# First stage in two sweeps with projections from split operands, and attention outputs folded in their own PSUM banks

## The chip, the core and the metric

The kernel runs on one core of a Trainium2 chip. The metric is the device time of one execution in microseconds (us). Five engines have a queue of instructions each and meet only at semaphores: TensorE (PE in the profile; PEld is its loading of the stationary operand), VectorE (DVE), ScalarE (ACT), GpSimd (POOL) and SyncE (SP), which here issues DMAs. An engine takes the instructions of its own queue in order.

## The reference

One encoder layer in float32, for 2048 tokens of width 1024. Only its first two parts matter here:

```
proj = x @ w_in                     # 1024 -> c_q 256, c_kv 128, k_r 32, and f, i, q, g of 512 each
# attention group: q = rms(c_q) @ w_uq, k and v = rms(c_kv) @ w_ukv, a rotary part of 32 shared by 8 heads,
#   softmax over the keys of the same or an earlier chunk of 64 tokens, times v (64 per head)
# recurrent group, 4 heads of 128: f = lb + (1-lb)*sigmoid(f), k = 1-f, and over chunks of tokens
#   o = causal (q k^T with decay) v + (q decay) state ;  state = decay*state + (k decay)^T v
#   r = rms(o) * silu(g)
```

After that come the output projection with a layer norm, a routing step, 45 blocks of a mixture of experts and a last layer norm. The change doesn't touch them.

## The kernel before

`build` (L1947) runs the stages one after the other. `phase_0` (L154) loads constants, computes the table `trig` of the rotary angles for all 2048 tokens, and issues the loads of the first 256 tokens of x and of `w_in` in five parts of columns. `phase_a` (L230) is the first stage, `phase_b` (L729) the attention; phases C to F are the rest. All engines meet at the end of each stage.

**Stage A** goes over 8 spans of 256 tokens. TensorE's order is written out by hand: in span m it projects i (`project_rows`, two tiles of 128 tokens with w_in as the moving operand of 512 columns), q (`project`, w_in stationary, 256 tokens moving), g (rows again), then the latent columns: c_kv, c_q (two parts) and k_r. Next it turns x of span m+1 (`turn_x`, 16 transposes into four PSUM banks, which ACT and DVE copy to `xT`), sums the squares of the latents with a matmul of ones (L403), and does the recurrence: scores (L411), the keys turned (L418), then `update`, `intra` and `inter` for each half of the span. The state is carried by DVE in eight steps, `chain` (L567), of four instructions each (L572); `inter` waits for them, and `rows` (L580) must free the one output bank O before the second `intra`. Between these waits `ahead` (L421) places pieces of the f projection of span m+1 (`project_f`, L335). The products are float32 matmuls, `wi` times `xT`.

ACT does the gates: sigmoid, log, exponentials, silu, and the roots. DVE does the cumulative sum in each chunk (L593, one scan of 1024 elements), the products with the exponentials (L616 to L622), the copies out of PSUM and the norms of the latents, whose reciprocal of 512 elements is L647. SP loads x of the next span into the only buffer `xt` once the present one is turned, and stores the recurrent output `ot`.

**Stage B** takes 64 steps, (head, pair of 128-query tiles). PSUM has four banks S for scores and for the projections of the next head's q, k and v (`prep_of`, L678), two banks T and two banks O. A step has units, one for two tiles of keys: `turn` transposes the probabilities into a T bank, ACT rounds them to float32r (`cast`, L949) and DVE takes the rest (`rest`, L1020), `weigh` multiplies both with the split values into O. `weigh` runs LAG = 4 units behind `turn`. When a step has been weighed, ACT copies O (`copy_o`, L956), and two units after the last weighing (FOLD_LAG = 2) `fold` (L894) turns the result back with a matmul, which adds the two halves of the split values. Its output takes its turn in the T banks (`T_ORDER`, `free_turn` L855), and DVE divides it by the row sums (`divide`, L1026). T_ORDER makes the next `turn` but one wait for DVE's `rest` of the unit just before the fold.

Of the kernel before, what the change touches and what calls it, by code (L numbers as in the profile page):

```python
# [58 lines left out]
W_PARTS = ((W_F, W_I), (W_I, W_Q), (W_Q, W_G), (W_G, W_COLS), (0, W_F))  # L59
# [38 lines left out]
def shape_constants():  # L98
# [19 lines left out]
    fold[:64, 64:] = (s[:64, None] % 32 == s[None, :64] % 32)  # L118
    fold[:, :64] = (s[:, None] % 64 == s[None, :64])
    c["fold"] = fold  # L120
    c["restart_tiles"] = np.tile((np.arange(NT * NE) % NT != 0).astype(np.float32), (P, 1))
# [6 lines left out]
    c["restart"] = np.tile((np.arange(HG * SPAN) % C != 0).astype(np.float32), (P, 1))  # L128
# [3 lines left out]
def lay_out(inputs):  # L132
# [12 lines left out]
    w = w[:, :, np.concatenate([np.arange(96), np.arange(80, 96), np.arange(64, 80)])]  # L145
# [8 lines left out]
def phase_0(nc, t, d):  # L154

    with ExitStack() as ctx:
        sb = lambda name, shape, dt=F32: ctx.enter_context(nc.sbuf_tensor(name, shape, dt))
        sem = lambda name: ctx.enter_context(nc.semaphore(name))
        pos_i = sb("pos_i", [P, SEQ], I32)
        ang = sb("ang", [P, SEQ])  # L160
        turns = sb("turns", [P, SEQ])
# [7 lines left out]
        with nc.Block() as block:  # L169
            @block.sync  # L170
            def _(sp):
                sp.dma_start(pos_i[:], d["positions"].broadcast_to([P, SEQ])).then_inc(loaded, 16)
                for dst, src in (
                    (t["ident"][:], d["ident"]), (t["causal"][:], d["causal"]), (t["fold"][:], d["fold"]),
                    (t["cols"][:], d["cols"]), (t["restart"][:], d["restart"]),
                    (lbl[:], d["hg_lb_logits"]), (t["gq"][:], d["q_norm_g"]),
                    (t["gkv"][:], d["kv_norm_g"]), (t["ghg"][:], d["hg_norm_g"]),
                ):
                    sp.dma_start(dst, src).then_inc(loaded, 16)
                sp.dma_start(t["xt"][:], d["x"][0].rearrange("(s i p) n -> s p i n", p=P, i=2)[0]).then_inc(t["x_loaded"], 16)  # L180

                w = d["w_in"].rearrange("(k p) n -> p k n", p=P)
                for (lo, hi), sem_ in zip(W_PARTS, t["w_in_loaded"]):
                    sp.dma_start(t["wi"][:, :, lo:hi], w[:, :, lo:hi]).then_inc(sem_, 16)
                sp.wait_ge(loaded, 160)

            @block.scalar
            def _(act):
                act.wait_ge(steps, 6)

                nc.scalar.activation(lbe[:], lbl[:], ACT.Exp).then_inc(act_steps, 1)
                act.wait_ge(steps, 15)
                nc.scalar.activation(t["trig"][:], ang[:], ACT.Sin).then_inc(act_steps, 1)

            @block.vector
            def _(v):
# [7 lines left out]
                step(v.tensor_copy(ang[:], pos_i[:]))  # L204
# [5 lines left out]
                col = lambda c: t["cols"][:, c:c + 1]  # L210

                step(v.tensor_scalar(ang[:], ang[:], col(C_INVF), None, ALU.mult))
                step(v.tensor_scalar(turns[:], ang[:], 1.0 / (2 * np.pi), col(C_TURN), ALU.mult, ALU.add))
                step(v.tensor_scalar(turns[:], turns[:], ROUND, None, ALU.add))
                step(v.tensor_scalar(turns[:], turns[:], -ROUND, None, ALU.add))
                for part in (PI2_A, PI2_B, PI2_C):
                    step(v.scalar_tensor_tensor(ang[:], turns[:], -part, ang[:], ALU.mult, ALU.add))
                step(v.tensor_scalar(ang[:], ang[:], col(C_RAD), None, ALU.add))
                step(v.tensor_scalar(ang[:], ang[:], 3.1415925, -3.1415925, ALU.min, ALU.max))
# [6 lines left out]
                v.wait_ge(act_steps, 2)  # L226
                step(v.tensor_scalar(t["trig"][:], t["trig"][:], col(C_SIGN), None, ALU.mult))

def phase_a(nc, t, d):  # L230

    with ExitStack() as ctx:
# [7 lines left out]
        wi = t["wi"]  # L240
        xt, x_loaded = t["xt"], t["x_loaded"]
        xT = sb("xT", [P, KT, SPAN])
# [3 lines left out]
        ep = sb("ep", [P, HG, SPAN])  # L246
        en = gate
# [8 lines left out]
        lmx = sb("lmx", [P, HG, NC + 1])  # L256
        gsum = sb("gsum", [P, HG, NC])
        gsum2 = sb("gsum2", [P, HG, NC])
        gf = sb("gf", [P, HG, NC])
        ssq = sb("ssq", [P, 2, HG])  # L260
        cqr = sb("cqr", [P, 3, SPAN])
        csq = sb("csq", [P, 3, SPAN])
        crs = sb("crs", [P, 2, SPAN])
# [4 lines left out]
        X = (U[2], U[3], B[2], B[0])  # L268

        x_turned = sem("x_turned"); xT_act = sem("xT_act"); xT_dve = sem("xT_dve")  # L270
        f_done = sem("f_projected"); i_done = sem("i_done"); q_done = sem("q_done"); g_done = sem("g_done"); c_done = sem("c_done")
        f_gate = sem("f_gate"); v_ready = sem("v_ready"); q_ready = sem("q_ready")
        g_ready = sem("g_ready"); c_raw = sem("c_raw"); c_sq = sem("c_sq"); kr_ready = sem("kr_ready")
# [20 lines left out]
        with nc.Block() as block:  # L294
            @block.sync
            def _(sp):
# [4 lines left out]
                def span(m, last):  # L301
                    if not last:

                        sp.wait_ge(x_turned, m * 4 + 4)
                        sp.dma_start(xt[:], xd[m + 1]).then_inc(x_loaded, 16)
# [3 lines left out]
                store(NS - 1)  # L309
# [3 lines left out]
            def _(pe):  # L313
                def turn_x(m, n):

                    if n == 0:
                        pe.wait_ge(x_loaded, m * 16 + 16)
                    for kk in range(2):
                        k = 2 * n + kk
                        for i in range(2):  # L320
                            ins = pe.transpose(X[n][:, kk * SPAN + i * P:kk * SPAN + (i + 1) * P],
# [3 lines left out]
                def project(out, col, m_cols):  # L325
                    for k in range(KT):
                        ins = pe.matmul(out, wi[:, k, col:col + m_cols], xT[:, k, :], start=(k == 0), stop=(k == KT - 1))  # L327
                    return ins

                def project_rows(b, i, col):  # L330
                    for k in range(KT):
                        ins = pe.matmul(b[:], xT[:, k, i * P:(i + 1) * P], wi[:, k, col:col + D_HG], start=(k == 0), stop=(k == KT - 1))
                    return ins

                def project_f(lo, hi):  # L335

                    for step in range(lo, hi):
                        h, part = divmod(step, 4)
                        for k in range(part * KT // 4, (part + 1) * KT // 4):
                            ins = pe.matmul(B[h // 2][:, h % 2 * SPAN:(h % 2 + 1) * SPAN], wi[:, k, W_F + h * P:W_F + (h + 1) * P],  # L340
                                            xT[:, k, :], start=(k == 0), stop=(k == KT - 1))
                        if step in (7, 15):
                            ins.then_inc(f_done, 1)
# [8 lines left out]

                for n in range(4):
                    turn_x(0, n)
                pe.wait_ge(t["w_in_loaded"][0], 16)
                pe.wait_ge(xT_act, 2)
                pe.wait_ge(xT_dve, 2)
                project_f(0, 16)

                def span(m, last):  # L360

                    def weights(part):
                        if is_first(m):
                            pe.wait_ge(t["w_in_loaded"][part], 16)
                    weights(1)
                    since(pe, state_ready, m * NC)
                    for i in range(2):
                        project_rows(U[i], i, W_I).then_inc(i_done, 1)
                    if not is_first(m):
                        turn_r(m - 1, 1)  # L370
                    weights(2)
                    for h in range(HG):
                        ins = project(U[2 + h // 2][:, h % 2 * SPAN:(h % 2 + 1) * SPAN], W_Q + h * P, P)
                        if h % 2:
                            ins.then_inc(q_done, 1)
                    weights(3)
                    if not is_first(m):
                        pe.wait_ge(r_out, m * 2)
                    project_rows(B[2], 0, W_G).then_inc(g_done, 1)
                    pe.wait_ge(f_gate, m * 4 + 2)  # L380
                    project_rows(B[0], 1, W_G).then_inc(g_done, 1)
                    weights(4)
                    pe.wait_ge(f_gate, m * 4 + 4)
                    project(B[1][:, 0:SPAN], W_CKV, P)
# [1633 lines left out]
```

## Time and profile before

| | us |
|---|---|
| median of 3 runs | 2718.45 (2716.57 to 2719.48) |
| the profiled execution | 2722.13, its span 2720.3 |
| stage A, its first matmul to stage B's first | 29.35 to 713.65 |
| stage B, to about | 1440 |
| share of the span: PE, PEld, DVE, ACT, POOL | 89%, 66%, 57%, 43%, 12% |
| TensorE clock, mean of the execution | 0.957 of full speed |

A row of a timeline gives start, length, engine, line, operation and the names it writes and reads, then a count when like instructions are merged, and in brackets the engine's idle time before it with what ended it. A float32 matmul of this kernel leaves two records of equal length in the trace, a float32r matmul one. Matmuls are pipelined, so the step from one start to the next, not the length of one, is what each costs.

### The profile page before, as it was taken

How to read it: one execution, taken by the hardware profiler on the slowest of the kernel's cores; microseconds unless marked ns; L12 is line 12 of the kernel's file. 1: busy time of each engine (PE TensorE's matmuls, PEld its weight loads, DVE VectorE, ACT ScalarE, POOL GpSimd, SP SyncE). 2: the span in 40 equal slices, each digit the busy share in tenths (PEclk: the TensorE clock that was granted, in tenths of full speed). 3: DMA queues.
4: the chain of work that ended last, by engine and by line, in shares of the span. 5: the costliest groups of instructions: out<-in, count | busy, mean ns of one | idle time of the engine just before them, and what ended most of it. 6: DMA issues, size and time to landing. Idle time of an engine off the chain costs nothing. (4 is left out here: it accounts for less than half of the span.)

```text
span 2720.3 us, 39975 instructions
## 1 busy us (share of the span) xinstructions
PE 2411.5 (89%) x12168; PEld 1804.8 (66%) x12169; DVE 1557.7 (57%) x2674; ACT 1157.7 (43%) x1903; POOL 317.3 (12%) x221
## 2 busy tenths in 40 slices
PE   5999999999799998999996999369999999999960
PEld 3776776766456566565664788258777788888840
DVE  3323444323476676776774444648787865656638
ACT  2222223122355565555663221046665644545433
POOL 0000000000000000000000111012333322222215
PEclk9999999999799999999997999589999999999985
DMA  5000000000000000000004322479999988878836
GB/s 208 16 24 8 23 23 15 23 8 8 22 7 5 8 13 6 9 12 6 9 6 143 118 93 93 145 287 359 309 376 312 334 292 278 268 229 276 291 69 247
DMA packets 148675, 338.23 MB, mean 124 GB/s; under 512 B 24672, under 2 KB 36576, under 8 KB 148320
## 3 DMA queue, kind: packets, MB, share of 16 engines
q1 hardware_dynamic: 135488, 289.45, 29.1%
q0 software_dynamic: 13104, 47.72, 7.2%
q8 instruction: 47, 0.77, 0.1%
q14 instruction: 36, 0.29, 0.0%
HBM read 288.38 MB, written 57.67 MB: 127 GB/s over the span
## 5 line engine op out<-in xcount | busy, mean ns | idle before, releaser
L1763 DVE TENSOR_TENSOR w_raw<-w_raw,w_hi 128x4096 f32 (+1 forms) x96 | 424.6, 4423 | 145.4 <-ACT w_hi L1754 145.4
L1754 ACT CAST w_hi<-w_raw 128x4096 fp32r (+1 forms) x96 | 347.7, 3634 | 122.3 <-DMA w_raw<-in_w 111.5
L1703 PE MATMUL eH<-w_hi,xh 128*128 128x512 f32 x720 | 290.6, 404 | 17.3 <-DVE xl L1821 17.3
L1704 PE MATMUL eH<-w_hi,xl 128*128 128x512 f32 x720 | 286.8, 398 | 0.0
L954 ACT CAST prT_hi<-pT 128x512 fp32r<-128x512 f32 (+1 forms) x288 | 162.1, 563 | 268.1 <-PE pT L871 268.0
L853 PE MATMUL pS<-kT,qT 128*128 128x512 f32 (+3 forms) x640 | 259.8, 534 | 5.4 <-ACT pr L946 4.9
L1023 DVE TENSOR_TENSOR prT_lo<-pT,prT_hi 128x512 fp32r<-128x512 f32 (+1 forms) x288 | 189.3, 659 | 123.6 <-ACT prT_hi L954 122.5
L1281 POOL TENSOR_TENSOR hp<-hp,b 128x1024 f32<-128x1024 f32 x16 | 40.7, 2546 | 1633.2 <-DVE hp L1336 1633.2
L1014 DVE TENSOR_REDUCE mx<-pS 128x1 f32<-128x512 f32 (+2 forms) x320 | 194.5, 610 | 24.4 <-PE pS L853 17.4
L1708 PE MATMUL eH<-w_raw,xh 128*128 x720 | 184.6, 398 | 4.2 <-DVE w_raw L1763 4.2
L853 PEld LDWEIGHTS pS<-kT,qT 128*128 128x128 f32 x640 | 111.0, 190 | 107.9 <-issue 72.5
L871 PE MATMUL pT<-ident,pr 128*128 128x128 f32 x832 | 152.0, 275 | 20.8 <-DVE prT_lo L1023 18.2
L327 PE MATMUL pu<-xT,wi 128*128 128x256 f32 (+1 forms) x768 | 170.4, 381 | 0.0
L1703 PEld LDWEIGHTS eH<-w_hi,xh 128*128 128x128 f32 x720 | 136.7, 190 | 50.3 <-issue 15.6
L1708 PEld LDWEIGHTS eH<-w_raw,xh 128*128 128x128 f32 x720 | 134.4, 188 | 41.1 <-issue 9.9
L946 ACT ACTIVATE pr<-pS,nmx 128x512 f32<-128x512 f32 (+1 forms) x240 | 153.5, 641 | 18.6 <-DVE nmx L1018 15.0
L1722 PE MATMUL eY<-w_hi,uh 128*128 128x512 f32 x360 | 147.5, 410 | 13.0 <-ACT w_hi L1754 13.0
L1704 PEld LDWEIGHTS eH<-w_hi,xl 128*128 128x128 f32 x720 | 136.9, 190 | 31.3
L327 PEld LDWEIGHTS pu<-xT,wi 128*128 128x128 f32 (+1 forms) x768 | 137.3, 181 | 30.7 <-issue 6.2
L1723 PE MATMUL eY<-w_hi,ul 128*128 128x512 f32 x360 | 143.7, 399 | 0.0
L871 PEld LDWEIGHTS pT<-ident,pr 128*128 128x128 f32 x832 | 101.4, 141 | 55.1 <-issue 38.6
L1662 POOL DMA_INDIRECT scratch_z<-y,sidx x45 | 134.1, 2980 | 22.1 <-issue 22.1
(291 smaller groups left out, 4242.0 us busy)
## 6 DMA issues: line engine op xcount, KB each, us to landing
w_raw<-in_w SPq DMA_DIRECT2D x96, 2048.0 KB
xt<-in_x SPq DMA_DIRECT2D x8, 1024.0 KB, 4.8
wi<-in_w_in SPq DMA_DIRECT2D x4, 2048.0 KB, 17.7
xs<-in_x SPq DMA_DIRECT2D x8, 1024.0 KB, 4.9
scratch_h<-hp SPq DMA_DIRECT2D x16, 512.0 KB, 3.0
fz<-scratch_z SPq DMA_DIRECT2D x16, 512.0 KB, 9.6
out<-fz SPq DMA_DIRECT2D x16, 512.0 KB, 2.6
scratch_rT<-ot SPq DMA_DIRECT2D x8, 512.0 KB, 2.9
```

Of the source, the lines that this page charges most:

```text
L327: ins = pe.matmul(out, wi[:, k, col:col + m_cols], xT[:, k, :], start=(k == 0), stop=(k == KT - 1))
L853: pe.matmul(b[:, 0:w], qT[:, x, at], kT[:, x, keys], start=True, stop=True).then_inc(scored, 1)
L871: ins = pe.transpose(b[:, m * P:(m + 1) * P], probs(n, i)[:, kt * P:(kt + 1) * P], t["ident"][:])
L946: nc.scalar.activation(probs(n, i)[:, j * 512:j * 512 + w], S[S_AT["score", (n, i, j)] % 4][:, 0:w], ACT.Exp, scale=SCALE, bias=nmx[:, til ...
L954: nc.scalar.copy(ph[:, u % RING, 0:w], T[T_AT["unit", u] % NTB][:, 0:w]).then_inc(t_hi, 1)
L1014: v.tensor_reduce(mx[:, tile % 4, j:j + 1], b[:, 0:w], AX, ALU.max).then_inc(mx_part, 1)
L1023: v.tensor_tensor(pl[:, u % RING, 0:w], T[T_AT["unit", u] % NTB][:, 0:w], ph[:, u % RING, 0:w].bitcast(F32), ALU.subtract).then_inc(t_lo, 1)
L1703: pe.matmul(H[:], xh[:, k, :], w.hi[:, k, :], start=(k == 0), stop=False)
L1704: pe.matmul(H[:], xl[:, k, :], w.hi[:, k, :], start=False, stop=False)
L1708: ins = pe.matmul(H[:], xh[:, k, :], lo[:, k, :], start=False, stop=(k == KT - 1))
L1754: nc.scalar.copy(w.hi[:], w.words(o).bitcast(F32)).then_inc(w.hi_ready, 1)
L1763: v.tensor_tensor(w.words(o), w.words(o).bitcast(F32), w.hi[:].bitcast(F32), ALU.subtract).then_inc(w.lo_ready, 1)
```

## The change

Stage 0 no longer computes `trig` nor loads the positions. It loads w_in without its 448 latent columns: f, i, q and g in two halves of 1 MB each. In stage A ACT rounds each part of w_in to float32r (`w_hi`) and DVE puts the rest in `w_lo`; x is split in the same way after each `turn_x`. A product of a k-tile is then three float32r matmuls, hi*hi + hi*lo + lo*hi. The latent projections leave the span: in span 7, ACT and DVE split the latent columns, loaded over those of f, and `ahead` makes the latents of span 0 there. A second sweep loads and turns x of spans 1 to 7 again, projects the latents into banks of its own, and there the angles are computed, a step in each turn. k_r is multiplied by `trig` at the end for all tokens.

In stage B one matmul makes the keys of two heads (128 columns where it was 64), for which the odd heads hold q and rotary parts in swapped halves of the partitions; `kT` gets four slots, and POOL copies the rotary keys to two of them. `fold` writes to columns 256 to 383 of its own O bank, one unit after the copy; `weigh` into an O bank waits for `divide` of the step two before.

```
-                for (lo, hi), sem_ in zip(W_PARTS, t["w_in_loaded"]):
-                    sp.dma_start(t["wi"][:, :, lo:hi], w[:, :, lo:hi]).then_inc(sem_, 16)
+                for (part, lo), sem_ in zip(W_PARTS, t["w_in_loaded"]):
+                    with sp.Fori(0, 2) as half:
+                        at = bass.ds(half * (KT // 2), KT // 2)
+                        sp.dma_start(t["w_lo"][part][:, at].bitcast(F32), w[:, at, lo:lo + D_HG]).then_inc(sem_, 16)
...
+                for j in range(1, NS):
+                    sp.wait_ge(x_turned, (NS + j) * 4)
+                    sp.dma_start(xt[:], xd[j]).then_inc(x_loaded, 16)
+                    if j == 1:
+                        store(NS - 1)
...
+                def project(out, w, cols, x, k):
+                    pe.matmul(out, wh[w][:, k, cols], xh[x][:, k, :], start=(k == 0), stop=False)
+                    pe.matmul(out, wh[w][:, k, cols], xl[x][:, k, :], start=False, stop=False)
+                    return pe.matmul(out, wl[w][:, k, cols], xh[x][:, k, :], start=False, stop=(k == KT - 1))
+                def project_rows(b, i, w):
+                    at = slice(i * P, (i + 1) * P)
                     for k in range(KT):
+                        pe.matmul(b[:], xh[0][:, k, at], wh[w][:, k, :], start=(k == 0), stop=False)
+                        pe.matmul(b[:], xl[0][:, k, at], wh[w][:, k, :], start=False, stop=False)
+                        ins = pe.matmul(b[:], xh[0][:, k, at], wl[w][:, k, :], start=False, stop=(k == KT - 1))
...
                     def ahead(lo, hi):
...
+                        if last:
+                            project_four(PAIR[0], C_COLS, 0, c_done, lo, hi)
+                        else:
+                            project_four(B[0:2], F_COLS, 0, f_done, lo, hi)
...
                 spans(pe, span)
+                pe.wait_ge(state_ready, NS * NC)
+                for n in range(4):
+                    turn_x(NS + 1, n, XC)
                 turn_r(NS - 1, 1)
+                for j in range(1, NS):
+                    if j < NS - 1:
+                        pe.wait_ge(xl_ready, (NS + j + 1) * 4)
+                        for n in range(4):
+                            turn_x(NS + j + 1, n, XC)
...
+                    project_four(PAIR[j % 2], C_COLS, j % 2, c_done, 0, 16)
+                    sums(j - 1)
+                sums(NS - 1)
...
+                def x_part(l, x, banks):        # ACT; DVE writes xl = bank - xh in the same way
+                    for n in range(4):
+                        act.wait_ge(x_turned, l * 4 + 1 + n)
+                        nc.scalar.copy(xh[x][:, 2 * n:2 * n + 2, :], banks[n][:].rearrange("p (k n) -> p k n", k=2)).then_inc(xh_ready, 1)
+                x_part(0, 0, X)
+                for part, w in enumerate("fiqg"):
+                    split_w(part, w, D_HG)
...
+                normalise(NS - 1)
+                v.wait_ge(sines, 1)
+                angle(11, v.tensor_scalar(t["trig"][:], t["trig"][:], col(C_SIGN), None, ALU.mult))
+                v.wait_ge(kr_ready, NS)
+                v.tensor_tensor(t["krp"][0:64], t["krp"][0:64], t["trig"][0:64], ALU.mult).then_inc(angles, 1)
...
-LAG, RING, FOLD_LAG = 4, 6, 2
+LAG, RING, FOLD_LAG = 4, 6, 1
...
-    return [(kind, h, c) for c in range(4) for kind in (("k", "q", "v") if h % 2 == 0 else ("k", "q"))]
+    return [(kind, h, c) for c in range(4) for kind in (("k", "q", "v") if h % 2 == 0 else ("q",))]
...
-                        ins = pe.matmul(b[0:64, :], wk[:, g, x, :], t["ckvn"][:, at], start=True, stop=True)
+                        ins = pe.matmul(b[:], wk[:, g], t["ckvn"][:, at], start=True, stop=True)
...
                 def turn(u):
-                    b = free_turn(T_AT["unit", u])
+                    if u >= NTB:
+                        pe.wait_ge(t_lo, u - NTB + 1)
+                    b = T[u % NTB]
...
                     if g == 0 and n >= 2:
-                        pe.wait_ge(o_copied, n - 1)
+                        pe.wait_ge(a_ready, n - 1)
...
                 def fold(n):
                     pe.wait_ge(o_copied, n + 1)
-                    b = free_turn(T_AT["fold", n])
                     for i in range(2):
-                        ins = pe.matmul(b[:, i * VD:(i + 1) * VD], oT[:, n % 2, i * P:(i + 1) * P], t["fold"][:, 0:VD], start=True, stop=True)
+                        ins = pe.matmul(O[n % 2][:, 2 * P + i * VD:2 * P + (i + 1) * VD], oT[:, n % 2, i * P:(i + 1) * P], t["stack"][:],
+                                        start=True, stop=True)
```

## Rows read from the trace of the kernel before

**Rows 1.** Windows, two stretches: busy time (instructions) of each engine, clock, DMA.
```profile
49.40:625.70 576.30, 576.30 (x3175) 414.00 (x3175) 211.62 (x456) 149.07 (x269) 0.00 (x0) 1.00 0.05 17
713.60:1440.00 726.40, 662.42 (x3464) 444.71 (x3464) 494.82 (x1249) 416.24 (x1097) 0.00 (x0) 0.99 0.04 9
```

**Rows 2.** Timeline of stage A: projection rows of span 0 and of span 7.
```profile
49.44 13.04 PE L332 MATMUL pu<-wi,xT 128*128 128x512 f32 x30
...
599.21 1.04 PE L321 MATMUL pu<-ident,xt 128*128 128x128 f32 x8
...
625.72 13.90 PE L332 MATMUL pu<-wi,xT 128*128 128x512 f32 x32
...
639.89 13.98 PE L327 MATMUL pu<-xT,wi 128*128 128x256 f32 x64
```

**Rows 3.** Timeline: float32r products in stage B (256 columns) and in the experts (512).
```profile
1003.69 0.48 PE L891 MATMUL pO<-prT_hi,v_split 128*128 128x256 f32 x2
1004.01 0.40 PE L891 MATMUL pO<-prT_lo,v_split 128*128 128x256 f32 x2
1004.25 0.60 PE L871 MATMUL pT<-ident,pr 128*128 128x128 f32 x4
...
2010.97 0.40 PE L1703 MATMUL eH<-w_hi,xh 128*128 128x512 f32 x1
2011.21 0.39 PE L1704 MATMUL eH<-w_hi,xl 128*128 128x512 f32 x1
```

**Rows 4.** The start: SP's issues of w_in (durations in ns, first and last start), then the timeline.
```profile
L184 SPq DMA_DIRECT2D wi<-in_w_in x5: 469/5004/7244, 5.9 to 19.8; - x5
...
27.53 1.29 DVE L227 TENSOR_SCALAR trig<-trig,cols 128x2048 f32<-128x2048 f32 x1 [1.03 <-ACT trig L193]
...
29.35 1.94 PE L321 MATMUL pu<-ident,xt 128*128 128x128 f32 x8 [29.35 <-PEq L169]
...
33.88 15.73 PE L340 MATMUL pb<-xT,wi 128*128 128x256 f32 x64 [0.88 <-DVE xT L557]
```

**Rows 5.** The page, part 5: splits of 4096 and of 512 elements; busy us, mean ns.
```profile
L1763 DVE TENSOR_TENSOR w_raw<-w_raw,w_hi 128x4096 f32 (+1 forms) x96 | 424.6, 4423 | 145.4 <-ACT w_hi L1754 145.4
L1754 ACT CAST w_hi<-w_raw 128x4096 fp32r (+1 forms) x96 | 347.7, 3634 | 122.3 <-DMA w_raw<-in_w 111.5
L954 ACT CAST prT_hi<-pT 128x512 fp32r<-128x512 f32 (+1 forms) x288 | 162.1, 563 | 268.1 <-PE pT L871 268.0
...
L1023 DVE TENSOR_TENSOR prT_lo<-pT,prT_hi 128x512 fp32r<-128x512 f32 (+1 forms) x288 | 189.3, 659 | 123.6 <-ACT prT_hi L954 122.5
```

**Rows 6.** The page, part 6: size and median time from issue to landing.
```profile
xt<-in_x SPq DMA_DIRECT2D x8, 1024.0 KB, 4.8
```

**Rows 7.** Timeline of the recurrence of span 6.
```profile
608.08 4.60 DVE L572 SCALAR_TENSOR_TENSOR state<-state,gf,pu 128x128 f32<-128x128 f32 x16 [3.15 <-PE pu L439]
...
618.10 1.13 DVE L587 SCALAR_TENSOR_TENSOR r_rows<-po,ssq,gin 128x128 f32<-128x128 f32 x4
...
619.78 1.05 PE L446 MATMUL po<-vt,am 128*128 128x128 f32 x8
```

**Rows 8.** Timeline of the change from stage A to B.
```profile
702.10 3.34 DVE L647 RECIPROCAL crs<-crs 128x512 f32<-128x512 f32 x1
...
713.65 7.05 PE L803 MATMUL pS<-krp,fold 64*64 64x512 f32 x8 [4.79 <-PEq L660]
```

**Rows 9.** Waits of TensorE in stage B: line, releaser, us in total, times, longest.
```profile
PE pT L871 <- DVE prT_lo L1023: 36.1, 68, 1.1
PE pT L898 <- DVE prT_lo L1023: 8.3, 28, 0.6
```

**Rows 10.** Timeline of stage B: a key projection and the next, a transpose after a fold.
```profile
725.73 1.07 PE L833 MATMUL pS<-ckvn,wk 128*64 128x512 f32 x2
726.73 1.98 PE L836 MATMUL pS<-cqn,wq 128*128 128x512 f32 x4
...
991.43 0.30 PE L871 MATMUL pT<-ident,krp 128*128 128x128 f32 x1 [0.78 <-DVE prT_lo L1023]
```

More of the change, by code:

```diff
@@ L245, in phase_a @@
         logf = sb("logf", [P, HG, SPAN])
-        ep = sb("ep", [P, HG, SPAN])
-        en = gate
+        ep, en = gate, logf
         qry = sb("qry", [P, HG, SPAN])
@@ L301, in span @@
                 def span(m, last):
-                    if not last:
-                        sp.wait_ge(x_turned, m * 4 + 4)
-                        sp.dma_start(xt[:], xd[m + 1]).then_inc(x_loaded, 16)
+                    sp.wait_ge(x_turned, m * 4 + 4)
+                    sp.dma_start(xt[:], xd[0 if last else m + 1]).then_inc(x_loaded, 16)
+                    if last:
+                        sp.wait_ge(f_done, 2 * NS)
+                        with sp.Fori(0, 2) as half:
+                            at = bass.ds(half * (KT // 2), KT // 2)
+                            sp.dma_start(wl["f"][:, at, 0:W_F].bitcast(F32), d["w_in"].rearrange("(k p) n -> p k n", p=P)[:, at, 0:W_F]).then_inc(
+                                t["w_in_loaded"][4], 16)
                     if not is_first(m):
@@ L392, in span @@
-                    if not last:
-                        turn_x(m + 1, 0)
-                        turn_x(m + 1, 1)
-                        pe.wait_ge(g_ready, m * 2 + 2)
-                        turn_x(m + 1, 2)
-                        turn_x(m + 1, 3)
-                    pe.wait_ge(c_raw, m * 3 + 3)
-                    pe.wait_ge(c_sq, m * 3 + 3)
-                    for n, (lo, hi) in enumerate(((0, 1), (1, 3))):
-                        for j in range(lo, hi):
-                            ins = pe.matmul(B[1][:, n * SPAN:(n + 1) * SPAN], t["ones"][:], csq[:, j, :],
-                                            start=(j == lo), stop=(j == hi - 1))
@@ L414, in span @@
                     for i in range(2):
-                        if not last:
-                            pe.wait_ge(xT_dve if i else xT_act, m * 2 + 3)
+                        pe.wait_ge(xl_ready, m * 4 + 5 + i)
                         for h in range(HG):
@@ L471, in span, with sums @@
                     ahead(12, 16)
+                def sums(j):
+                    pe.wait_ge(c_raw, 3 * j + 3)
+                    pe.wait_ge(c_sq, 3 * j + 3)
+                    b = PAIR[j % 2][0]
+                    for n, (lo, hi) in enumerate(((0, 1), (1, 3))):
+                        for k in range(lo, hi):
+                            ins = pe.matmul(b[:, n * SPAN:(n + 1) * SPAN], t["ones"][:], csq[:, j % 2, k, :], start=(k == lo), stop=(k == hi - 1))
+                    ins.then_inc(c_sum, 1)
@@ L723 @@
 S_AT = {e: n for n, e in enumerate(S_ORDER)}
-T_ORDER = [e for s in range(SLOTS + 1) for e in ([("unit", s)] if s < NU else []) + ([("fold", FOLD_SLOT[s])] if s in FOLD_SLOT else [])]
-T_AT = {e: n for n, e in enumerate(T_ORDER)}
 NTB = 2
@@ L978, in _ @@
                                     copy(p)
+            @block.gpsimd
+            def _(pool):
+                pool.wait_ge(rope_copied, 8)
+                for x in range(2):
+                    half = slice(64 - 64 * x, 128 - 64 * x)
+                    nc.gpsimd.tensor_copy(kT[half, 2 + x], kT[half, x]).then_inc(rope_again, 1)
             @block.vector
@@ L1032, in divide @@
                     v.reciprocal(rin[:, both], rin[:, both]).then_inc(rin_ready, 1)
+                def divide(n):
+                    both = slice(2 * n, 2 * n + 2)
                     v.wait_ge(rin_ready, n + 1)
```

390 lines of the change are left out of this document (222 added, 168 removed).

## The prediction

> **What bounds the kernel now.** I read the windows first, one for each stage the diff touches. In the first, spans 0 to 6 of stage A, TensorE is busy for 576.30 of 576.30 us at full clock, while DVE is busy for 37% and ACT for 26% [rows 1]. So stage A is bound by what TensorE streams, and each column saved there comes off the end. In stage B it is busy for 662.4 of 726.4 us, DVE for 495, ACT for 416 [rows 1]: TensorE bounds it too, but 64 us of it are waits. The timeline then gives the price of a product. A span starts with the i projection; span 0's is at 49.44 and span 7's at 625.72 [rows 2], so a span takes 82.3 us. A record of 512 columns costs (13.90 - 0.59) / 31 = 0.429 us and one of 256 (13.98 - 0.38) / 63 = 0.216 [rows 2] (0.59 and 0.38 being the length of one), and a float32 product has two.
>
> **The span, part by part.** Before: i and g are 64 records of 0.429 = 27.5 us; q, f, c_kv and c_q 176 of 0.216 = 38.0; k_r 16 of 0.22 = 3.5; the sums of squares 6 of 0.216 = 1.3. That leaves 82.3 - 70.3 = 12.0 for transposes and recurrence, which stay.
>
> After: each product is three float32r ones. The trace has them. With 512 columns the step from start to start is 2011.21 - 2010.97 = 0.235 us [rows 3], three of them 0.70 for 0.86 before. With 256 columns, four products in stage B start between 1003.69 and 1004.25: the two first take 0.32, the two last 0.24 [rows 3], so a step is 0.12 in the stream and at most 0.20 behind another operation. 0.12 is half of 0.235, so I take 0.118; the bounds are 0.118 and 0.20. Then i and g are 96 x 0.235 = 22.5, q and f 192 x 0.118 = 22.7, and a span is 22.5 + 22.7 + 12.0 = 57.2 us.
>
> What ran beneath the longer products must still fit. The tightest place is the recurrence. In span 6 DVE's `rows` for the first half ended at 619.23, and TensorE came to `intra` at 619.78 behind two blocks of five steps of `ahead` [rows 7]. Each block shrinks from 4.3 to 3.5 us, so TensorE comes 1.6 us earlier and DVE is late by 0.8 us, less what it gains from starting earlier: it is the first thing late. I take 0.9: 58.1 a span. Splitting x costs four casts of 0.56 on ACT and four subtractions of 0.66 on DVE [rows 5], one bank behind the other, in place of two copies on each; the last is done some 2.7 us after the last transpose, beneath the scores and turned keys (2.7 us), with `ahead` right behind: nothing to a microsecond a span. DVE loses the 3.34 us reciprocal [rows 8] in each span, so its load stays near 30 us of 58. The scan in four pieces, the exponentials written over `gate` and `logf`, and the one wait more of ACT fall beneath the i and q projections, 23 us before `scaled` is wanted; without that cover each would cost under 1 us a span.
>
> **The start.** Before, DVE's angles end the stage at 28.8 us, PE starts at 29.35 and f at 33.88 [rows 4]. Without them the queue of SP is the last: five issues take until 24.8 us, the later ones 5.0 each [rows 4], and with one part less it is free at about 19. The barrier then lets PE turn x from 19.3 (cold, 3.9 us); ACT rounds x and then w_in's f (two halves of 2048 elements at 3634 / 4096, 1.8 each), DVE subtracts (2.2 each) [rows 5], one after the other: f starts at 30.5. This is 3.4 us of the 10 won; the rest goes to the splits. At half clock at first, as before (15.7 us for 13.8 [rows 4]), f takes 13.1: span 0 starts at 43.6, where it was 49.44. Splits of i, q and g run beneath f and i. Bounds: f between 26 and 34.
>
> **Spans 0 to 7** end at 43.6 + 7 x 58.1 + 61.1 = 511.4. The last has 3 us more: between silu and x, ACT and DVE split the latent columns (1.6 and 1.9 twice), and the turned keys and `ahead` wait for the x behind them. Its `ahead` makes the latents of span 0, so the recurrence that stood almost bare before is covered.
>
> **The second sweep.** TensorE turns x again (16 records of 0.11 [rows 2] = 1.8 us) and projects 96 x 0.118 = 11.3, with sums of 1.3: 14.5 a turn, against 6 us of ACT and at most 11 of DVE, which both run a turn ahead. But the first is bare. x of span 2 can be fetched only when span 1 is out of `xt`, and behind `store(7)`, which waits for the last r; nothing but `turn_r` is left for TensorE. r is out some 2.5 us after, the load takes 4.8 [rows 6]: 8 us idle, and 2.5 more for the cold clock after it. The tail is bare too: raws and sums of span 7 (3 us), roots, two normalisations (3.34 [rows 8] + 1.4 each, the first beside the roots), `trig` by its sign 1.29 [rows 4], and k_r by trig for 2048 elements, 2.2 at DVE's rate [rows 5]. It comes to 16 us from the last projection to the barrier, and all that the angles cost at the end is 4. Sum: 1.8 + 8 + 2.5 + 7 turns of 14.5 + 16 = 129.8, so stage B starts at 641 instead of 713.65 [rows 8]: 72 us won.
>
> **Stage B.** 32 key projections become 16. A pair of records with 64 columns took 726.73 - 725.73 = 1.00 us [rows 10]; one with 128 takes 2 x 0.429. 32.0 - 13.7 = 18.3 us of TensorE, of which I count 15, since each bank is now held by two copies. The fold leaves the T banks. Of 36.1 us in which `turn` waits for DVE [rows 9], I read the part behind a fold, like the 0.78 at 991.43 [rows 10], as the larger, and it goes, for `turn` may then be two units ahead again; the 8.3 us of the fold's own waits [rows 9] turn into waits of `turn` for the same event. What is late next is ACT's chain of cast and exp, busy for 57% of the stage [rows 1]. I take 20, between 0 and 36. Against it: fold follows the copy of O by one unit (0.9 us) instead of two, and at steps of one unit `weigh` waits for `divide`; behind those waits stand the next turns. 4 us, between 0 and 15. Stage B: 31 us, between 5 and 50. POOL's two copies of 2048 elements are wanted first at head 2, over 100 us later, and POOL has nothing else: nothing.
>
> **Sum.** The profiled execution took 2722.1, the span 2720.3 of it. 2722.1 - 72 - 31 = 2619; the median of the runs lies 3.7 lower, so I forecast 2616.
>
> **A rule that speaks against the change.** In stage B the four products follow each other by 0.12 although each loads 128 columns of its own [rows 3], so here the load is hidden. The Trainium skill (TensorE: Matmul & The Clock Gate, "The mechanism" in part 3) says that a load overlaps matmuls in flight only where its row group differs, which it never does in these products. By that rule the trace should not show 0.12; its consequence is the last rival's.
>
> **The rivals.**
> - Stage B gives little: ACT and DVE set the pace of `turn`, the waits at the fold move one unit on, and only the keys gain some 7 us: 2640. For it: 28 waits of the fold itself were for the same DVE operation [rows 9]. Against: DVE is busy for 68% of the stage [rows 1].
> - The spans don't follow TensorE: in each, the split of x by two engines in turn, or the recurrence, leaves it 4 us idle more, a span is 62 and the clock may fall in places: 2616 + 8 x 4 = 2648. For it: the 0.55 us that TensorE came after DVE [rows 7]. Against: DVE is busy half the span.
 At 0.20, the first step of each group [rows 3], the 96 x 2 x 8 + 96 x 8 = 2304 products of q, f and the latents cost 0.082 more each, 189 us: 2805. From 0.163 on the kernel is slower than before. Against: there is no wait in front of the later steps, and they stay at 0.12.
> - The change does not do what it says (a float32r product in more than one pass, as a float32 one): excluded by one record of 0.235 for 512 columns [rows 3].
>
> **How the numbers follow.** Forecast 57% (2600 to 2633), little from B 15%, slow spans 15%, slower 5%; 8% for more than I count, from the fold and from shorter waits, near 2590. Range 2588 to 2660. A measurement can tell 0.2%, 5.4 us. Faster 94%, within it 1%, slower 5%.
>
> **What would show it.** Right: in stage A q's records 0.118 apart; i to i 58 us; a gap of 8 us before the second sweep's second turn; stage B's first matmul near 641; its length near 695, with hardly a wait of L871 behind a fold. Wrong: 256-column steps of 0.14 or more (each 0.01 is 23 us), spans over 60, waits for xT_lo or for `state`, or a stage B over 715.

## The result, and the profile after

| | before | after |
|---|---|---|
| median of the runs, us | 2718.97 (2716.57 to 2725.64, 4 runs) | 2585.77 (2584.25 to 2590.62, 4 runs) |
| profiled execution, span, us | 2720.3 | 2583.8 |
| stage A: TensorE's first record to stage B's first matmul | 29.35 to 713.65 | 21.20 to 636.28 |
| stage B: first matmul to the stage's last instruction | 725.3 | 666.4 |
| from there to the end of the span | 1281.4 | 1281.1 |

The ratio is 0.9509 (95%: 0.9489 to 0.953): 4.9% faster. The time forecast was 2616 us in a range from 2588 to 2660; it came out 30 us lower and 2 us below the range, in the case to which the prediction gave 8% ("near 2590"). The last row says that nothing changed behind stage B, so all of it is in two places: stage B's first matmul is 77.4 us earlier (forecast 72), and stage B is 58.9 us shorter (forecast 31).

The windows of the changed kernel, which answer to [rows 1]: the eight spans, the second sweep with its tail, stage B.
```profile
core 0: us, PE busy (x) PEld busy (x) DVE busy (x) ACT busy (x) POOL busy (x), PEclk, DMA share, GB/s
45.80:508.70 462.90, 458.32 (x3838) 413.68 (x3838) 219.01 (x530) 161.68 (x266) 0.00 (x0) 1.00 0.09 33
...
508.70:636.20 127.50, 105.59 (x838) 103.18 (x836) 72.66 (x72) 40.35 (x100) 0.00 (x0) 0.94 0.16 55
636.20:1302.40 666.20, 629.86 (x3432) 442.27 (x3432) 482.56 (x1248) 418.53 (x1097) 3.77 (x2) 0.99 0.04 10
```
The first sweep is as full of TensorE as before: 4.6 us of 462.9 are idle, 3.8 of them in one place (below). The second sweep is the stretch with holes: 22 us of 127.5. Stage B has 36 us idle where it had 64.

The timeline of the products, answering to [rows 2, 3]: the last of `f` and the first of `i` in span 0, then the `i` that begins span 1 and the one that begins span 7.
```profile
45.50 0.28 PE L325 MATMUL pb<-xT_hi,wf_hi 128*128 128x256 f32 x1
...
45.74 0.29 PE L327 MATMUL pb<-xT_hi,wf_lo 128*128 128x256 f32 x1
45.87 0.39 PE L332 MATMUL pu<-wi_hi,xT_hi 128*128 128x512 f32 x1
46.09 0.39 PE L333 MATMUL pu<-wi_hi,xT_lo 128*128 128x512 f32 x1
...
102.73 0.40 PE L332 MATMUL pu<-wi_hi,xT_hi 128*128 128x512 f32 x1
...
445.99 0.39 PE L332 MATMUL pu<-wi_hi,xT_hi 128*128 128x512 f32 x1
```
A product of 256 columns steps by 0.12 us, also in a run of 96 with a load of its own for each; one of 512 by 0.229 (38 steps from 45.87 to 54.58). From `i` to `i` it is (445.99 - 45.87) / 7 = 57.2 us. Read the length column with care: a record is 0.28 long, but the step from start to start, 0.118, is what the product costs.

The start, answering to [rows 4]: SP's last two issues of `w_in` (one line: start of the first, time to the end of the second), TensorE's first transposes, its first product.
```profile
13.91 6.65 SPq L185 DMA_DIRECT2D wg_lo<-in_w_in  x2
...
21.20 1.94 PE L319 MATMUL pu<-ident,xt 128*128 128x128 f32 x8 [21.20 <-PEq L169]
...
31.94 0.55 PE L325 MATMUL pb<-xT_hi,wf_hi 128*128 128x256 f32 x1 [7.09 <-DVE wf_lo L610]
```
SP is free at 13.91 + 6.65 = 20.6 us, and the barrier opens 0.6 later, at 21.20.

The recurrence in span 0, answering to [rows 7], and the one wait in the first sweep, in the last span: turned keys behind the split of x.
```profile
96.11 1.13 DVE L642 SCALAR_TENSOR_TENSOR r_rows<-po,lg,gin 128x128 f32<-128x128 f32 x4
...
97.29 1.16 PE L434 MATMUL po<-vt,am 128*128 128x128 f32 x8
...
486.92 1.31 PE L406 MATMUL pu<-ident,key 128*128 128x128 f32 x8 [3.29 <-DVE xT_lo L603]
...
489.11 0.41 PE L326 MATMUL pb<-xT_lo,wf_hi 128*128 128x256 f32 x1
489.32 0.41 PE L327 MATMUL pb<-xT_hi,wf_lo 128*128 128x256 f32 x1
```
DVE's `r_rows` ends at 97.24 and TensorE's `intra` starts at 97.29, 0.37 us behind the product before it (96.92). In all eight spans this step is 0.37 to 0.38 us; where TensorE changes from such a product to another operation without a wait, it is 0.21 (91.05 to 91.26). So TensorE does wait for `rows` in each span, but only for some 0.2 us.

The second sweep's start, and its tail with the first matmul of stage B, answering to [rows 8].
```profile
508.75 1.91 PE L319 MATMUL pu<-ident,xt 128*128 128x128 f32 x16
...
518.72 3.59 PE L319 MATMUL pu<-ident,xt 128*128 128x128 f32 x16 [7.63 <-DMA xt<-in_x]
...
620.10 2.75 PE L467 MATMUL pb<-csq,ones 128*128 128x256 f32 x12
...
622.46 3.35 DVE L705 RECIPROCAL crs<-crs 128x512 f32<-128x512 f32 x1 [9.28 <-ACT crs L578]
...
627.04 3.35 DVE L705 RECIPROCAL crs<-crs 128x512 f32<-128x512 f32 x1
...
631.62 1.28 DVE L746 TENSOR_SCALAR trig<-trig,cols 128x2048 f32<-128x2048 f32 x1
632.94 2.28 DVE L748 TENSOR_TENSOR krp<-krp,trig 64x2048 f32<-64x2048 f32 x1
636.28 2.04 PE L892 MATMUL pS<-krp,fold 64*128 64x512 f32 x2 [13.43 <-PEq L751]
```
Behind the last sums DVE works through two reciprocals, their normalisations, the sign and the multiplication, all of it in front of the barrier: 13.4 us with TensorE idle.

The waits of TensorE in stage B, answering to [rows 9] (the turn is at L953 now, the fold at L979).
```profile
PE pS L892 <- PEq L751: 13.4, 1, 13.4
PE pT L953 <- DVE prT_lo L1118: 10.4, 37, 0.3
PE pT L953 <- ACT pr L1032: 8.8, 7, 1.9
PE pS L921 <- ACT pr L1032: 5.0, 6, 1.1
...
PE pO L973 <- DVE a_out L1134: 1.8, 3, 0.6
```
The first row is the hole in front of the stage again; of the others, the turn's waits for DVE fell from 36.1 to 10.4 us, and the fold has no row left. And one fold with its neighbours, before (the fold waits, and the turn at 991.43 behind it waits again) and after:
```profile
990.02 0.63 PE L898 MATMUL pT<-fold,oT 128*128 128x64 f32 x4 [0.22 <-DVE prT_lo L1023]
```
```profile
887.50 0.40 PE L973 MATMUL pO<-prT_lo,v_split 128*128 128x256 f32 x2
887.73 0.55 PE L979 MATMUL pO<-stack,oT 128*128 128x64 f32 x4
888.12 0.28 PE L953 MATMUL pT<-ident,krp 128*128 128x128 f32 x1
```
After: the turn starts 0.39 us behind the fold's start. Before: 1.41 us (991.43 in [rows 10] less 990.02). In the ring it is the very next `turn`, not the next but one, that waits for the `rest` of the unit just before the fold: `free_turn` looks two entries back, and one of the two is the fold.

That wait is the rule and not one example. Of the 68 waits of the turn for DVE before, 36 stand right behind a fold, of 27.5 us together and up to 1.15 each; the other 32 make 8.6 us, none over 0.32. After, none of the 37 stands behind a fold, and none is over 0.32.

### The profile page after: what moved, and what is told of

Read it like the earlier page. It is cut to its first block and busy times, and to the rows that moved or that the text cites. A ratio compares the mean times of both kernels' runs of the same rounds, so it can differ in the third digit from the quotient of the medians.

```text
span 2583.8 us, 42394 instructions
## 1 busy us (share of the span) xinstructions
PE 2292.1 (89%) x13288; PEld 1857.2 (72%) x13289; DVE 1595.6 (62%) x2749; ACT 1203.5 (47%) x1969; POOL 310.9 (12%) x223
## 5 line engine op out<-in xcount | busy, mean ns | idle before, releaser
L1802 PEld LDWEIGHTS eH<-w_hi,xh 128*128 128x128 f32 x720 | 136.6, 190 | 47.9 <-issue 15.3
L953 PE MATMUL pT<-ident,pr 128*128 128x128 f32 x832 | 151.3, 274 | 7.7 <-DVE prT_lo L1118 4.9
L1380 POOL TENSOR_TENSOR hp<-hp,b 128x1024 f32<-128x1024 f32 x16 | 40.7, 2545 | 877.6 <-DVE hp L1435 877.6
L325 PE MATMUL pb<-xT_hi,wf_hi 128*128 128x256 f32 x448 | 131.7, 294 | 8.6 <-DVE wf_lo L610 7.1
L973 PE MATMUL pO<-prT_hi,v_split 128*128 128x256 f32 x576 | 135.1, 315 | 1.8 <-DVE a_out L1134 1.8
L953 PEld LDWEIGHTS pT<-ident,pr 128*128 128x128 f32 x832 | 102.5, 142 | 36.0 <-issue 23.5
```

The costliest lines, as they stand in the source:

```text
L953: ins = pe.transpose(b[:, m * P:(m + 1) * P], probs(n, i)[:, kt * P:(kt + 1) * P], t["ident"][:])
L1802: pe.matmul(H[:], xh[:, k, :], w.hi[:, k, :], start=(k == 0), stop=False)
```

## Experiments

Stage A came out near its forecast, so most runs are on stage B. The expectations weigh two explanations of its 59 us. Theory 1: what cost so much was the fold's place in the ring of two T banks, since at each fold TensorE stopped twice, once at the fold and once at the next turn; the bank is worth over 40 us and the key projections some 17. Theory 2: the bank is worth what was counted (20 - 4 = 16 us), and the rest comes from something else, such as the new order on DVE or the fold's new moment. All kernels are versions of the changed one unless said otherwise; "ratio" is always to the kernel before, run beside it, and lengths of stage B are from the profiles.

**1. The fold back in the T ring, two units behind the copy of O, with the reciprocal inside the division; key projections and all of stage A as changed.**
```diff
-LAG, RING, FOLD_LAG = 4, 6, 1
+LAG, RING, FOLD_LAG = 4, 6, 2
...
-                    if u >= NTB:
-                        pe.wait_ge(t_lo, u - NTB + 1)
-                    b = T[u % NTB]
+                    b = free_turn(T_AT["unit", u])
...
+                    b = free_turn(T_AT["fold", n])
                     for i in range(2):
-                        ins = pe.matmul(O[n % 2][:, 2 * P + i * VD:2 * P + (i + 1) * VD], oT[:, n % 2, i * P:(i + 1) * P], t["stack"][:],
+                        ins = pe.matmul(b[:, i * VD:(i + 1) * VD], oT[:, n % 2, i * P:(i + 1) * P], t["stack"][:],
```

> The fold takes its turn in the T banks again, two units after the last weighing, with the row sums inverted just before the division, as in the kernel before; keys of two heads at once stay. Theory 1 (the fold as a third user of two banks was the cost, and what the trace shows as idle there leaves out the drain of the matmul ahead): stage B goes from 666 us to about 710, the kernel from 2586 to 2630, and waits of L871's kind behind a fold come back. Theory 2 (the forecast's sizes were right for the fold, 16 us net, and the keys gave the rest): stage B about 682, the kernel 2602.

Measured: 2624.99 us, ratio 0.9655 (0.9627 to 0.9684). Stage B takes 707.1 us, 40.7 more. The waits of the kernel before are back:
```profile
PE pT L963 <- DVE prT_lo L1129: 35.7, 68, 1.1
PE pT L990 <- DVE prT_lo L1129: 11.3, 28, 1.3
```
35.7 in 68 waits of the turn, as 36.1 in 68 in [rows 9]. Theory 2's 16 us is out.

**2. Key projections one head at a time, 64 columns each; the rest as changed.**
```diff
-                        ins = pe.matmul(b[:], wk[:, g], t["ckvn"][:, at], start=True, stop=True)
+                        ins = pe.matmul(b[x * 64:x * 64 + 64, :], wk[:, g, x * 64:x * 64 + 64], t["ckvn"][:, at], start=True, stop=True,
+                                        tile_position=(0, x * 64))
...
```

> Keys of one head per matmul again, 64 columns, 32 projections instead of 16, nothing else. Theory 1: 17 us of TensorE's time come back, and little more: stage B 681 to 685, the kernel about 2602. Theory 2 (the keys gave the rest, because fewer users of the S banks take waits away too): stage B 700 or more, the kernel 2620.

Measured: 2600.83 us, ratio 0.9568 (0.9545 to 0.9591). Stage B takes 684.0 us, 17.6 more.
```profile
636.80:1320.90 684.10, 653.79 (x3464) 443.18 (x3464) 483.60 (x1249) 417.71 (x1097) 3.77 (x2) 0.99 0.04 9
```
Against the last row of the windows above, TensorE is busy for 23.9 us more and idle for 6 less. With the first run's 40.7 that makes 58.3 of 58.9 us.

**3. The own bank on the kernel before, with nothing else of the change.** (Its ring entries for folds go, the fold comes one unit behind the copy of O, the reciprocal ahead of it.)
```diff
-LAG, RING, FOLD_LAG = 4, 6, 2
+LAG, RING, FOLD_LAG = 4, 6, 1
...
-        O = [psum(f"pO{i}")[:, 0:2 * P] for i in range(2)]
+        O = [psum(f"pO{i}") for i in range(2)]
...
-                    b = free_turn(T_AT["unit", u])
+                    if u >= NTB:
+                        pe.wait_ge(t_lo, u - NTB + 1)
+                    b = T[u % NTB]
```

> The kernel before, with only the fold of the attention outputs changed: own bank, one unit after the copy, row sums inverted early. Theory 1 (the T banks): stage B is 38 to 45 us shorter than 725 and the kernel takes 2676 to 2681. Theory 2 (it needs the keys' share of the S banks to get there): 2695 or more.

Measured: 2672.37 us, ratio 0.9836 (0.9819 to 0.9852). Stage B takes 679.0 us, 46.3 less than before, a little over the 38 to 45 expected.
```profile
PE pT L861 <- DVE prT_lo L1012: 10.5, 37, 0.3
```
```profile
710.80:1389.90 679.10, 650.23 (x3464) 440.62 (x3464) 483.44 (x1249) 411.91 (x1097) 0.00 (x0) 0.99 0.04 10
```
The other half of the reading is in the second fence. The kernel before, over its stage B, reads
```profile
713.60:1438.60 725.00, 662.42 (x3464) 444.71 (x3464) 494.53 (x1248) 416.24 (x1097) 0.00 (x0) 0.99 0.04 9
```
with the same 3464 instructions. Of the 45.9 us between the two rows, 33.7 come out of the idle time (62.6 to 28.9) and 12.2 out of *busy* time, with no instruction less. The same holds for experiment 1 against the changed kernel: of 41.0 us between the two windows (x3432 both), 11.9 are busy time. As I read it, the length of a record reaches past the step to the next (0.28 for 0.118 in the stream), and only the last record before a wait shows all of it: there a part of the loss stands in the busy column, and no row of the waits has it. An estimate agrees in size: the waits of the stage go from 119 to 61, and 58 x (0.28 - 0.118) = 9.4 us. No run tests it apart.

**4. Own bank, but the fold one unit later, ahead of `weigh`.**
```diff
-LAG, RING, FOLD_LAG = 4, 6, 1
+LAG, RING, FOLD_LAG = 4, 6, 2
...
-                            if LAG <= s < NU + LAG:
-                                weigh(s - LAG)
                             if s in FOLD_SLOT:
                                 fold(FOLD_SLOT[s])
+                            if LAG <= s < NU + LAG:
+                                weigh(s - LAG)
```

> The fold keeps its own bank but comes one unit later, between the transposes and the weighing of that unit. If leaving the T banks is what counts, stage B stays within 3 us of 666. If the earlier place of the fold counts (it fills a gap in which DVE catches up), stage B is 10 us or more longer.

Measured: 2603.26 us, ratio 0.9573 (0.9552 to 0.9594). Stage B takes 684.2 us, 17.8 more, with a new wait at the head:
```profile
PE pO L973 <- DVE a_out L1134: 11.6, 10, 2.0
PE pT L953 <- DVE prT_lo L1118: 10.6, 40, 0.3
```
The turn's waits stay at 10.6, so the ring is not touched. But the own bank couples the fold to `weigh`: the next `weigh` into this O bank needs the division done, and a fold one unit later leaves it too little time. The moment matters once the bank is shared. The size is that of the expectation's second branch, but the reason is another than the one it gave. `weigh` waits 9.8 us more for the division than in the changed kernel (1.8), and of the 18.1 us between the two windows 9.5 again stand as busy.

**5. Fold in the T ring, but at the new moment, with the early reciprocal.** The edit is against the kernel of experiment 1.
```diff
-LAG, RING, FOLD_LAG = 4, 6, 2
+LAG, RING, FOLD_LAG = 4, 6, 1
...
                     both = slice(2 * n, 2 * n + 2)
-                    invert(n)
...
+                            if s in COPY_SLOT:
+                                invert(COPY_SLOT[s])
```

> The fold in the T banks, but one unit after the last weighing, and the row sums inverted early as in the changed kernel. If the T banks are the cost, stage B is 35 to 45 us longer than 666. If the place of the fold and the order of DVE are, it is within 10 us of it.

Measured: 2635.65 us, ratio 0.9691 (0.9672 to 0.971); stage B 714.3 us, 47.9 more (35 to 45 expected).
```profile
PE pT L963 <- DVE prT_lo L1129: 38.9, 65, 2.2
PE pT L990 <- DVE prT_lo L1129: 11.9, 16, 2.8
```
The moment and the order alone bring nothing; in the ring they are worse by 7 us than the old ones. With moment and order held as in the changed kernel, the bank alone is worth these 47.9 us. Bank and moment are one edit.

**6. The reciprocal of the sums back inside the division.**
```diff
                 def divide(n):
                     both = slice(2 * n, 2 * n + 2)
+                    invert(n)
...
-                            if s in COPY_SLOT:
-                                invert(COPY_SLOT[s])
```

> The changed kernel with the row sums reduced and inverted just before the division again instead of a unit earlier. If the order on DVE is part of the gain of stage B, it loses 5 us or more; if the banks and the place of the fold are all, less than 2.

Measured: 2589.49 us, ratio 0.9524 (0.9508 to 0.954); stage B 672.0 us, 5.6 more in the profile. The two kernels' times overlap (2587.02 to 2592.71 against 2584.25 to 2590.62), so the size is not clear of the noise: the profiles say 5.6 us and the medians 3.7. It is a small part of the 59 at most.

**7. Stage A in two sweeps, but with one float32 product where the change has three.** It leaves out the low parts: only the high parts are multiplied, as float32, which costs what the full float32 product costs.
```diff
-                    pe.matmul(out, wh[w][:, k, cols], xh[x][:, k, :], start=(k == 0), stop=False)
-                    pe.matmul(out, wh[w][:, k, cols], xl[x][:, k, :], start=False, stop=False)
-                    return pe.matmul(out, wl[w][:, k, cols], xh[x][:, k, :], start=False, stop=(k == KT - 1))
+                    return pe.matmul(out, wh[w][:, k, cols].bitcast(F32), xh[x][:, k, :].bitcast(F32), start=(k == 0), stop=(k == KT - 1))
...
```
`project_rows` is changed in the same way.

> Each product of stage A is one float32 matmul of the rounded parts w_hi and xT_hi read as float32; the two products with the low parts are left out, the splits and everything else of the changed kernel stay. Theory 1 (the streaming of the products makes the gain of stage A): a span is 64 x (0.429 - 0.344) + 128 x (0.216 - 0.177) = 10.4 us longer, the latents 2.5, so stage B starts at 636 + 8 x 12.9 = 739 us, later than in the kernel before (713.7), and the kernel takes 2689. Theory 2 (much of it comes from the two sweeps, that is from the start without angles and the recurrence that is covered in the last span): stage B starts before 713.

Measured: 2680.29 us, ratio 0.9851 (0.9827 to 0.9876). Spans last 67.0 us, and stage B starts at 732.64.
```profile
114.05 13.90 PE L330 MATMUL pu<-wi_hi,xT_hi 128*128 128x512 f32 x32
...
181.03 9.18 PE L330 MATMUL pu<-wi_hi,xT_hi 128*128 128x512 f32 x21
```
```profile
732.64 2.04 PE L888 MATMUL pS<-krp,fold 64*128 64x512 f32 x2 [13.43 <-PEq L747]
```
So the cheaper products bring 732.6 - 636.3 = 96.4 us, and the two sweeps by themselves cost 713.65 to 732.64 = 19.0. Their 77.4 us is a difference of two larger numbers. The 19 us is itself a balance: the two holes (7.8 us at the start of the second sweep in this run, 13.4 where 4.8 stood) cost 16 us and the second turning of x in seven spans another 12, while the earlier start (`i` at 47.52 for 49.44) and the last span, whose recurrence now has products between its steps, give part back. The runs don't price these last terms one by one.

**8. A better version: the holes of stage A filled.** Three edits: the turning of the x of span 2 moves from the start of the second sweep to behind projection 1; the latent columns of w_in are split one step earlier in the last span, not between silu and x; sine and sign, roots and normalisation of span 6 and the first seven eighths of `krp` times `trig` move ahead of the last projection.
```diff
-                    if j < NS - 1:
+                    def turn_next():
+                    if 1 < j < NS - 1:
+                        turn_next()
...
+                    if j == 1:
+                        turn_next()
...
+                    if last:
+                        split_w(4, "f", W_F)
...
+                    if j == NS - 1:
+                        v.wait_ge(kr_ready, NS - 1)
+                        at = slice(0, (NS - 1) * SPAN)
+                        v.tensor_tensor(t["krp"][0:64, at], t["krp"][0:64, at], t["trig"][0:64, at], ALU.mult).then_inc(angles, 1)
```

> A version that may beat the changed kernel: (a) in the second sweep x of span 2 is turned behind the latents of span 1 instead of ahead of them, so that its load lies beneath them; (b) the latent columns are split behind the values' copies in span 7, not between the silu and x; (c) angles and the sine a turn earlier, sums and norms of span 6 ahead of the latents of span 7, k_r times trig for seven spans before the tail. Theory 1 (the three places where the trace of the changed kernel shows TensorE idle, 7.6, 3.8 and 13.4 us, are independent): a wins 6 us (a wait for the last r of 2.5 stays), b 3.8, c 6: stage B starts at 620, the kernel takes 2570. Theory 2 (each idle place moves to the next dependency): stage B starts at 630 or later.

Measured: 2570.70 us (2568.05 to 2576.97), ratio 0.946 (0.9441 to 0.9479): 15 us under the changed kernel, whose lowest run was 2584.25, and the fastest here.
```profile
507.34 0.35 PE L325 MATMUL pb<-xT_hi,wf_hi 128*128 128x256 f32 x1 [1.90 <-DVE xT_lo L614]
...
522.15 1.46 PE L467 MATMUL pb<-csq,ones 128*128 128x256 f32 x6
527.38 2.59 PE L319 MATMUL pu<-ident,xt 128*128 128x128 f32 x16 [3.78 <-DMA xt<-in_x]
```
```profile
612.62 2.01 DVE L760 TENSOR_TENSOR krp<-krp,trig 64x1792 f32<-64x1792 f32 x1
...
623.06 0.41 DVE L764 TENSOR_TENSOR krp<-krp,trig 64x256 f32<-64x256 f32 x1
624.53 2.04 PE L908 MATMUL pS<-krp,fold 64*128 64x512 f32 x2 [6.96 <-PEq L767]
```
The wait in the last span is gone (its sweep ends at 503.10 in place of 508.75: 5.7 us), and the gap in front of stage B is 6.96 in place of 13.43: 6.5. The head of the second sweep gave next to nothing: in place of 7.63 us TensorE waits 1.90 for the split of span 1's x, which the hole had covered, and 3.78 for the x of span 3. That load can start only when the late turning has emptied the one buffer for x, and then just the sums are left to cover it. Behind each of these two waits, too, products of 256 columns step by 0.21 for a while (508.2 to 511.4 and 530.0 to 531.7). Stage B starts 11.8 us earlier; the other 3 of the 15 us are spread over the later stages, within what these vary from kernel to kernel (1278.9 us behind stage B here, 1281.1 in the changed kernel, 1285.4 in experiment 7). That the expected 2570 us was met so exactly is luck: of the three places one gave nothing, stage B came at 624.5 for 620, and the later stages made up for it.

## Why the prediction was wrong, by its own steps

- **What bounds the kernel**: held. TensorE set stage A in both sweeps but for the holes (4.6 us idle of 462.9 in the first).
- **The price of a product**: held for 256 columns (0.118 taken and measured). 512 columns cost 0.229 for 0.235 (the rows as printed give 0.24), which is 22.0 us a span for 22.5. The experiment with float32 products gives a span 9.8 us longer; the prediction's terms for i, g, q and f say 27.5 + 27.6 - 22.5 - 22.7 = 9.9. The rival in which products of 256 columns don't pipeline in long chains is refuted by the 2304 of them.
- **The rule that speaks against it**: a new load in each product, one every 0.12 us (the rows at 45.50 and 45.74, two steps apart), and TensorE does not wait for it. The Trainium skill (TensorE: Matmul & The Clock Gate, "The mechanism" in part 3) has a load overlap matmuls in flight "only when row_grp differs"; here it never does, and the trace does not agree with that sentence of the page.
- **The recurrence stall of 0.9 us a span**: came as some 0.2 us. I take DVE's earlier start, which the prediction named and did not count, for the rest; no run isolates it. With the cheaper products of 512 columns: 57.2 for 58.1, 6.6 us over seven spans.
- **The start**: 31.94 for 30.5. The prediction had the queue of SP free at about 19 (24.8 less one issue of 5.0 is 19.8); it was at 20.6, and the barrier opened at 21.20 for 19.3. From there turning and splits took 10.7 us for 11.2. Then f took 13.9 for 13.1, since its products stepped by 0.213 until 37.4. Span 0's `i` came at 45.87 for 43.6.
- **The last span**: the 3 us of its splits came as 3.3 and 0.5 us, in the place named. The span took 62.8 us for 61.1; a little over 1 us of that is the lower clock behind the wait, for which there was no term.
- **The second sweep**: 127.5 us for 129.8. Hole of 7.63 for 8, cold start 1.7 (3.59 for 1.91) for 2.5, tail 16.2 for 16. These are terms of bare waits read off single rows, and all are within a microsecond.
- **Stage A in sum**: 2.3 - 6.6 + 1.7 - 2.3 = -4.9, so 4.9 us better than forecast.
- **Stage B, the keys**: 15 counted, 17.6 measured against the changed kernel.
- **Stage B, the fold: this is the step that failed.** The prediction said "I take 20, between 0 and 36", less 4, so 16. Taking the fold out of the ring, with its new moment and the early reciprocal, is worth 40.7 us with the new keys and 46.3 with the old ones. Four errors add up to it, here with the numbers of experiment 3. First, the turn's 36.1 us of waits for DVE fell by 25.6 where 20 were counted (5.6): the reading that the part behind a fold is the larger was right, but that part is 27.5 us, and one example at 991.43 could not give its size. Second, "the 8.3 us of the fold's own waits ... turn into waits of `turn` for the same event": they did not (8.3). Without an entry for the fold each turn takes the bank of the unit two before it, and the turn's waits that were not behind a fold grew only from 8.6 to 10.5. Third, 12.2 us stood as busy, where no row of waits shows them, so that the upper bound of 36 was too low as well. Fourth, of the 4 us against it 1.8 came, as `weigh`'s wait for the division (2.2). 5.6 + 8.3 + 12.2 + 2.2 = 28.3, and 16 + 28.3 = 44.3 stands beside the measured 46.3; the last 2 us I don't place.
- **Stage B, the other edits**: no term but POOL's copies, at nothing. Experiments 2 and 3 both have the fold in its own bank and one head per key projection, and stage B takes 684.0 and 679.0 us. The 5.0 us between them are the stage's other edits (swapped halves, four slots of `kT`, POOL's copies, the wider rotary matmuls), or the spread of single profiles, for that of experiment 3 was of its fastest run, 6 us under its median. With these 5.0 counted, the stage adds up: 46.3 + 17.6 - 5.0 = 58.9.
- **The range**: stage B's upper bound of 50 us stood on the same 36, and 58.9 were measured. With 12 us more for the fold the low end would have been 2576.

What stays open: why the own bank is worth 46.3 us in the kernel before and 40.7 in the changed one, and which of stage B's other edits costs the 5 us, if it is one of them. And whether the x of span 2, turned in the middle of projection 1, would close the second sweep's start was not tried.

## What to carry to other kernels

When an operation shares a small ring of banks with a stream of others, its cost is the waits in front of it and behind it, and the part of each that is drawn as busy: compare steps from start to start with and without it, and take the idle time listed for it as a lower bound. Moving it to a bank with another partner removes that cost only if the new partner's release comes early enough, so move its moment and its releaser in the same edit. In a stage that has been made dense, the new holes are at its ends, and they are cheap to find beforehand: two of the three filled here were worth 12 us.

## What the runs showed of the hardware

- A float32r product of 512 columns steps by 0.229 us in a run of 48 (45.87, 46.09 and on), against the 0.235 read off [rows 3]; of 256 columns by 0.118 in runs of up to 96, with a load for every product.
- Behind the idle gaps of 7.6 and 3.3 us the granted clock is 0.53 and 0.52, the lower level (1.2 GHz of 2.4; it is the third number from the end in the windows below). 16 transposes took 3.59 us at 518.72 for 1.91 at 508.75. Behind the wait of 3.3 us in the last span the products of 256 columns stepped by 0.213 for 2.5 us, in place of 0.118. The prediction had no term for the second, and it came to a little over 1 us.
- At the start the same products step by 0.213 from 32.3 to 37.4 us, as at the lower level, while the profile puts the granted clock of 31.9 to 36.0 at 1.00. There the step shows the price, and the clock row does not.
- Time lost to a wait shows partly as busy: 12.2 of 45.9 us in stage B (experiment 3) and 11.9 of 41.0 (experiment 1), with the number of instructions unchanged.

The windows of the changed kernel behind these two gaps:
```profile
488.70:491.50 2.80, 2.74 (x12) 2.63 (x12) 1.15 (x2) 0.15 (x1) 0.00 (x0) 0.52 0.00 0
518.70:522.30 3.60, 3.58 (x18) 3.60 (x19) 1.51 (x3) 1.76 (x3) 0.00 (x0) 0.53 0.00 0
```
